# Transposing the probabilities at the head of a slot of the prompt attention instead of at its end

## What is computed

```python
s_c = einsum('btghd,bngd->bghtn', q, k_c) * scale + bias_c      # 32 compressed blocks
o_c = einsum('bghtn,bngd->btghd', masked_softmax(s_c), v_c)
# the selected keys: of 1024 prompt keys in blocks of 64, 16 blocks, so all up to the query
s_s = einsum('btghd,bgtkld->bghtkl', q, k_g) * scale + bias_s
# the window: the last 512 keys
o_w = einsum('bghts,bsgd->btghd', masked_softmax(q k^T * scale + bias), v)
o = g[0] * o_c + g[1] * o_s + g[2] * o_w                        # sigmoid gates
```

## Time and profile before

| | |
|---|---|
| median of 3 runs | 2355.3 us |
| lowest and highest | 2349.26 and 2356.98 us |
| profiled execution | 2354.62 us |
| its span, first to last instruction | 2353.0 us |
| PE busy over the span | 2128.4 us, 90% |
| mean granted TensorE clock | 0.944 |
| stage `prompt_attention` | about 436 to 978 us |

### The profile page before, as it was taken

One profiled execution on the slowest core, in us unless ns is written; L12 is line 12 of the kernel. 1 busy time (PEld: TensorE's weight loads), 2 busy tenths in 40 slices (PEclk: granted clock), 3 DMA queues, 4 the chain that ended last, 5 costly groups with the idle time before them and its releaser, 6 DMA issues. The chain is left out here.

```text
span 2353.0 us, 36411 instructions
## 1 busy us (share of the span) xinstructions
PE 2128.4 (90%) x14280; PEld 1439.2 (61%) x14280; DVE 852.0 (36%) x1636; ACT 694.6 (30%) x1279; POOL 330.6 (14%) x245
## 2 busy tenths in 40 slices
PE   3888966799999999897699979895999999999998
PEld 2446634577777777664366756563666666666666
DVE  4211051455555555455432544334222222222223
ACT  5212231245454545326142233212211111211121
POOL 3200032400000000000102111102510410411400
PEclk7898978899999999898799989996999999999999
DMA  5421352111111111201110155302111111111101
GB/s 207 127 71 46 128 149 71 49 50 43 55 38 56 55 47 38 74 23 36 38 45 9 63 145 151 134 12 54 45 54 45 53 48 50 45 53 45 53 27 74
DMA packets 189719, 153.31 MB, mean 65 GB/s; under 512 B 9169, under 2 KB 176231, under 8 KB 189291
## 3 DMA queue, kind: packets, MB, share of 16 engines
q1 hardware_dynamic: 180170, 138.96, 19.6%
q0 software_dynamic: 4640, 10.60, 1.7%
q10 hardware_dynamic: 4800, 2.30, 0.3%
HBM read 124.66 MB, written 31.33 MB: 66 GB/s over the span
## 5 line engine op out<-in xcount | busy, mean ns | idle before, releaser
L416 PE MATMUL ps<-hH,wH 128*128 128x352 f16 x1536 | 318.3, 317 | 47.7 <-ACTq L389 27.8
L416 PE MATMUL ps<-hL,wH 128*128 128x352 f16 x1536 | 317.5, 316 | 0.0
L416 PE MATMUL ps<-hH,wL 128*128 128x352 f16 x1536 | 316.5, 315 | 0.0
L403 DVE SCALAR_TENSOR_TENSOR wL<-w,wH 128x1024 f16<-128x1024 f32 x98 | 120.1, 1225 | 323.8 <-ACT wH L396 308.3
L416 PEld LDWEIGHTS ps<-hH,wH 128*128 128x128 f16 x1536 | 151.4, 99 | 132.8 <-issue 48.5
L416 PE MATMUL ps<-mH,wH 128*128 128x352 f16 x960 | 195.9, 313 | 8.4 <-DVEq L389 6.9
L416 PEld LDWEIGHTS ps<-hL,wH 128*128 128x128 f16 x1536 | 152.1, 99 | 82.1
L416 PEld LDWEIGHTS ps<-hH,wL 128*128 128x128 f16 x1536 | 151.7, 99 | 81.3
L416 PE MATMUL ps<-mL,wH 128*128 128x352 f16 x960 | 195.9, 313 | 0.0
L416 PE MATMUL ps<-mH,wL 128*128 128x352 f16 x960 | 195.9, 313 | 0.0
L485 PE MATMUL ps<-hH,wH 128*128 128x352 f16 x576 | 181.0, 314 | 2.0 <-ACT cmpT L497 0.8
(11 more groups left out here) (409 smaller groups left out, 2929.3 us busy)
## 6 DMA issues: line engine op xcount, KB each, us to landing
w<-in_mlp_w SPq DMA_DIRECT2D x64, 512.0 KB, 3.9
w<-in_w_in SPq DMA_DIRECT2D x32, 512.0 KB, 3.9
gates<-cmpT SPq DMA_DIRECT2D x24, 528.0 KB, 3.0
hH<-gates SPq DMA_DIRECT2D x24, 528.0 KB, 3.5
paw<-in_w_in SPq DMA_DIRECT2D x24, 512.0 KB, 4.7
hL<-in_w_branch SPq DMA_DIRECT2D x24, 256.0 KB, 3.8
xTd<-xT SPq DMA_DIRECT2D x1, 4224.0 KB
xT<-xTd SPq DMA_DIRECT2D x1, 4224.0 KB, 13.0
```

The lines of the kernel that those rows point to most:

```text
L403: self.k.nc.vector.scalar_tensor_tensor(self.k.wL[:, slot % 2, :, :], self.k.w32[:, slot, :, :], WS, self.k.wH[:, slot % 2, :, :], ALU.mul ...
L416: ins = nc.tensor.matmul(k.ps[:, 3 * parity + c, 0:CH], w[:, kt, :], x[:, kt, c * CH:(c + 1) * CH], start=(kt == 0 and x is inH and w is w ...
```

## The change

In PE's stream the transposes, which were the last thing of a slot, become the first. The jobs that each part of slot j works on stay the same.

```diff
--- before.py
+++ after.py
@@ -1228,13 +1228,13 @@
                 for g in range(G):
                     pe.wait_ge(q_low[g], 1)
                 for j in range(NJ + LEAD):
+                    if 2 <= j < NJ + 2:
+                        turn(j - 2)
                     if j < NJ:
                         score(j)
                     if j >= LEAD:
                         fill.multiply(pe, PIECES[(j - LEAD) % 8][0])
                         values(j - 4)
-                    if 2 <= j < NJ + 2:
-                        turn(j - 2)
 
             @block.sync
             def _(sp):
```

## The result

| | before | changed |
|---|---|---|
| median, 12 runs each | 2352.44 us | 2365.61 us |
| lowest and highest | 2346.31 to 2361.29 | 2362.21 to 2375.80 |
| span of the profiled execution | 2353.0 us | 2363.1 us |

The ratio is 1.0061, with a 95% interval of 1.0044 to 1.0079: slower by 0.6%, clear of no change. The medians differ by 13.2 us, the two profiled spans by 10.1 us.

What follows compares the result with a forecast made beforehand. The prediction took PE's own instruction stream to bound the kernel. Its terms 9.4 + 3.8 + 1.3 + 0.3 = 14.8 us, added to the profiled execution's 2354.6, gave 2369.4 us, with a range of 2361 to 2378.

Steps and rivals of the forecast that it cites:

- work term: PE's stream: no instruction added or removed, the same transposes, scores, values and gate matmuls, so 0.
- Part 2, the bank: Transposes wait for ACT's copy, queued behind the gate evacuation, to free PSUM bank 4 or 5: stalls 9.4 + 3.8 us.
- restart: After a stall in 12 window slots the first weight load can't have run ahead: 0.11 us each, 1.3 us.
- Part 1, the exponentials: PE's transposes of job j-1 need its exponentials; ACT's idle time of 0.50 us covers the wait, so 0.
- Part 3, the ends: Slots 2 and 3: transposes now stand ahead of scores that ACT and DVE wait for, at clock 0.50: 0.3 us.
- C's price: Expectation for ACT's copies put first: the late evacuation holds the next gate matmuls, a wait of 5 us or more.
- The covers hold: Rival, 8%: copies come free early enough at the transposes, no change, 2355 us.
- The clock falls: Rival, 5%: PE's granted clock drops after back-to-back selected values and transposes in some 12 slots, 30 us lost, 2399 us.
- Part 1's wait bites: Rival, 3%: late exponentials use up the 0.50 us reserve in 48 short slots, 0.1 us lost each, 2374 us.
- The gap before compressed values closes: Rival, 4%: idle PE loads before value matmuls, 21.9 us, are an unseen copy wait and go: 2332.7, or 2347.5 with stalls.

Runs made afterwards that it cites:

- kernel with the copies ahead: Changed kernel with ACT's copies of job j-2 put ahead of the gate evacuation within a slot: median 2348.60 us, ratio 0.9983 to the kernel before.
- narrow evacuation: Changed kernel with the evacuation cut to the first 88 of 352 columns: median 2354.11 us, ratio 1.0012 to the kernel before.
- second instruction: Changed kernel with an unread second ACT instruction of 352 columns behind each evacuation: median 2374.48 us, ratio 1.0083 to the kernel before.
- run with zeros: Kernel before, with compressed-value products taking a 128-row tile of zeros and 128 rows of other values: median 2333.35 us, ratio 0.9906.

## Why the prediction was right

It said 2369.4 us, slower by 0.6% against the median shown; measured were 2365.61 us and 0.6%. The mechanism, the places and the size of the stalls were right. That the two percentages agree is in part luck: the sum of 14.8 us was some 5 us too large, for the reason given under the work term, and the two profiled executions differ by 10.1 us, 0.4%.

**Part 2, the bank.** Held in place and number, and in size to 0.3 us. The chain was put at 1.45 us from the last gate matmul to the free bank, and the transposes came at 1.52 to 1.53 in all 23 slots. By the starts the stalls are 11 x 0.92 + 4 x 0.54 + 8 x 0.32 = 14.8 us, where the text had 9.4 + 3.8 and 1.3 for the restart, 14.5. The 0.07 that I missed lies between the copy's end and the transpose: in slot 97 the load starts 0.10 and the matmul 0.13 us behind the copy's end, where the sum had 0.05. I had taken a restart of 0.11 in window slots alone, because in compressed ones load and matmul begin together anyway; the 0.07 is in both. So the total is closer than its parts: 10.1 for 9.4 in the compressed slots, 4.7 for 3.8 + 1.3 in the window slots. The kernel with the copies ahead shows that this is all one cause: with the evacuation behind them every stall is gone.

**Part 1, the exponentials.** Held: only the 3.3 us at the start show up again, 3.5 us.

**Part 3, the ends.** From the first scores to the first gate matmul of the stage it was 435.99 to 441.13, 5.14 us, and is 435.74 to 441.29, 5.55 us. That is 0.4 for a forecast of 0.3, but this stretch can't tell: it is 5.53 us with the narrow evacuation and 6.52 with the second instruction, two kernels whose orders up to there are those of the changed one. So part 3 is neither shown nor refuted.

**The work term of 0 was wrong.** This is the step that failed, by some 5 us. In the changed kernel a pass has 3.94 us of stall and is only 2.60 longer, so the new order gives 1.3 us a pass back. With the stalls taken away it beats the kernel before: 131.95 against 133.16 us a pass, 1.2 less (and 0.14 of C's price in it). The transposes have other neighbours, and I had counted instructions and not neighbours. Before, five transposes stood behind compressed values, and took 0.61 us (704.03 to the scores at 704.64), where behind window values they take 0.56 (776.55 to the scores at 777.11):

```profile
704.64 0.28 PE L1203 MATMUL ps<-w,oH 128*128 128x128 f16 x2
...
777.11 0.70 PE L1203 MATMUL ps<-w,oH 128*128 128x512 f16 x3
```

What follows the first of them comes 0.05 late, 16 times in a pass, 0.8 us. The run with zeros shows that the few rows of the values are the cause: in the order of before, it has none of these delays. With the change a single, narrow transpose stands there, the next instruction is hardly late, and 0.7 of the 0.8 us is gone. The rest, 0.6 us a pass, are late starts that I find by comparing the two traces slot by slot. The first gate matmuls of slots 60, 63 and 66, behind evacuations, start 0.37 us earlier in sum, most of it too little for the idle column (3.8 us in 12 places before, 3.4 in 9 with the change). Once a pass, in slot 72, window values come 0.27 us earlier: their idle loads of 0.36 us are in the 21.9 us of the earlier trace rows and missing in the 18.9 us of the changed kernel, which has one for each of the 64 compressed jobs. No run takes these two away by themselves, so where they are is shown and why they go is not.

The same step is behind the opening statement that a change of order can gain at most the 7 us of listed waits: the distances between two starts depend on the neighbours as well, and no list of waits shows them. So the sum should have read 14.8 + 0.4 - 5.3 = 9.9 us. The two spans differ by 10.1, the medians by 13.2; runs of one kernel lie 14 us apart, so this difference between the two is not something to explain.

**The rivals.** "The covers hold" fell with the new wait. "The clock falls" fell: 1.00 in the two windows above, with stalls of 0.92 us and runs of 8 transposes in them. So what the Trainium skill, TensorE: Matmul & The Clock Gate, "A second HAM failure mode: psum-queue depth-cycling", says of small idle times did not show here. "Part 1's wait bites" did not happen. "The gap before compressed values closes" did not happen (0.29 us in slot 97, before and after), and the run with zeros shows why it couldn't: the gap was never a wait for the copies. But what stands behind the gap, which the prediction priced only as a wait, was worth more than the change: 21 us.

## What to carry to other kernels

In a pipeline over slots written by hand, an operation that moves a slot ahead on one engine must be checked against the order of every engine that frees its buffers: here ACT's queue had an evacuation in front of the copy, which cost next to nothing as long as the transposes were late anyway. The stalls of such an edit come out to within 0.1 us a slot, by laying the releasing chain (0.35 + 0.46 + 0.59, and the step to the other engine) against the arrival of the waiting engine, kind by kind of job. What the instructions cost beside new neighbours is a term of its own, here a third of the stalls. When the orders of two engines depend on one another, try them in pairs: 1.006 and 1.023 for each alone, 0.998 together.

## What the runs showed of the hardware

A float32 product with few rows (4 to 32) between products of 128 rows is dear, not cheap. Its first weight load begins 0.24 us after the start of the last gate matmul (703.67 after 703.43), while the load for that gate matmul ran beside the one before it, in the same trace:

```profile
703.28 0.31 PE L485 MATMUL ps<-hL,wH 128*128 128x352 f16 x1
703.28 0.10 PEld L485 LDWEIGHTS ps<-hH,wL 128*128 128x128 f16 x1
```

From the last gate matmul over its two matmuls to the next transpose it took 0.60 us, with the same two matmuls over 128 rows 0.32 us. By the starts, and alike for 4 to 32 rows, each of the three steps is longer: 0.24 instead of 0.15 us to the first matmul, 0.16 instead of 0.06 to the second, 0.20 instead of 0.11 to the transpose. The instruction behind that transpose is 0.05 us late as well.

The Trainium skill, TensorE: Matmul & The Clock Gate, "Step-by-step: what each phase is for", says that TensorE pulls a weight load ahead of running matmuls if the row groups don't conflict or it goes to the background buffer, and that the number of rows doesn't matter for a load's time. The load's length agrees (groups of loads of before: mean 182 ns for 8 rows and more, 198 for 4, and 191 for 128). On the pulling ahead the section doesn't say which load goes to the background buffer; in these runs loads of 128 rows were pulled ahead of a running matmul of 128 rows, and loads of 4 to 32 rows were not.

The second observation is on ScalarE: what stood behind an evacuation of 352 columns started 0.45 us after it in every slot of the changed kernel, although the evacuation's record is 0.55 long, and behind one of 88 columns 0.23 with 0.33. So what counts in a queue is the distance of starts, and for the last instruction of the chain its end.
